# One transfer queue, two deadlines: the down part of an expert asked for behind the gate and up parts of the next

## The reference

```python
# MOE_EXPERTS = 32, MOE_TOP_K = 2, MOE_FF = 256, D_MODEL = 1024
combine = jnp.einsum('tk,tke->te', w, jax.nn.one_hot(flat_idx, MOE_EXPERTS))
gate = jnp.einsum('td,edf->tef', t, w_gate)      # w_gate (32, 1024, 256)
up   = jnp.einsum('td,edf->tef', t, w_up)        # w_up   (32, 1024, 256)
hid  = jax.nn.silu(gate) * up * combine[:, :, None]
out  = jnp.einsum('tef,efd->td', hid, w_down)    # w_down (32, 256, 1024)
```

## Times and profile before

| | us |
|---|---|
| median of 3 runs | 1007.43 |
| the 3 runs | 1004.38, 1007.43, 1034.75 |
| the profiled execution, its own time | 1007.99 |
| its span in the trace | 1005.8 |

### The profile page before, as it was taken

The page is one execution under the profiler, slowest core; times in us unless marked ns, Lnnn a source line. Parts: engine busy times, 40 slices in busy tenths (PEclk is TensorE's granted clock), DMA queues, the critical chain, the costliest instruction groups (busy, mean ns, idle before and its releaser), DMA issues.

```text
span 1005.8 us, 15290 instructions
## 1 busy us (share of the span) xinstructions
PE 961.0 (96%) x5525; PEld 577.3 (57%) x5525; DVE 512.6 (51%) x936; ACT 306.6 (30%) x599; POOL 217.9 (22%) x267
## 2 busy tenths in 40 slices
PE   7999999999989999998999999999999998999986
PEld 5544444444546656667666665576655555555552
DVE  2366446444865555556567776573333332333327
ACT  3220002222544434432232233133333333333313
POOL 2200000222600750001233332002222222222003
PEclk9999999999999999998999999999999999999999
DMA  9996523000000000005011114987999999999748
GB/s 324 359 353 223 208 92 53 0 1 0 7 0 1 1 1 1 2 1 210 1 64 63 63 64 190 410 317 251 371 418 404 403 400 384 417 415 405 267 181 334
DMA packets 55072, 192.54 MB, mean 191 GB/s; under 512 B 15370, under 2 KB 26706, under 8 KB 39506
## 3 DMA queue, kind: packets, MB, share of 16 engines
q1 hardware_dynamic: 46644, 173.10, 45.2%
q0 software_dynamic: 7056, 18.36, 4.8%
q10 hardware_dynamic: 1296, 0.07, 0.1%
HBM read 174.21 MB, written 24.64 MB: 198 GB/s over the span
## 4 chain that ended last, share of the span: by engine, by line
PE 43%; DMA 6%; DVE 3%; issue 1%; ACT 1%; SPq 0%; ACTq 0%; POOL 0%; DVEq 0%; POOLq 0%
PE PS L1671 13%; PE PS L1540 11%; PE PS L1697 7%; DMA ring<-in_w_down_dram 3%; PE PS L1646 2%; PE PS L1464 1%; PE PS L1562 1%; PE PS L1508 1%; DMA ring<-in_w_gate_dram 1%; PE PS L1728 1%; DMA y_g<-y_rows 1%; PE PS L1523 1%; PE PS L1680 1%; PE PS L1552 1%; DVE y_sum L2311 1%
## 5 line engine op out<-in xcount | busy, mean ns | idle before, releaser
L1671 PE MATMUL PS<-ring,xg_T 128*64 x736 | 162.7, 379 | 3.5 <-ACT near_gu L1857 2.6
L1671 PE MATMUL PS<-near_gu,xg_T 128*64 128x256 f32 x736 | 162.7, 379 | 0.0
L1671 PEld LDWEIGHTS PS<-ring,xg_T 128*64 128x64 f32 x736 | 100.7, 137 | 63.0 <-issue 16.3
L1540 PE MATMUL PS<-w_out_sb,cat_T 128*128 128x512 f32 x256 | 118.0, 603 | 1.4 <-DVE y_sc L2006 1.0
L1012 PE MATMUL PS<-hT,w_x 128*128 128x512 f32 x256 | 112.0, 594 | 0.0
L435 POOL TENSOR_SCALAR rstd<-stat 128x1 f32<-128x1 f32 (+1 forms) x48 | 22.3, 465 | 368.8 <-ACT junk L615 181.3
L1671 PEld LDWEIGHTS PS<-near_gu,xg_T 128*64 128x64 f32 x736 | 100.7, 137 | 0.0
L1697 PE MATMUL PS<-ring,hid_T 128*64 x184 | 83.8, 598 | 0.4 <-DVE hid_T L2253 0.4
L1697 PE MATMUL PS<-near_dn,hid_T 128*64 128x512 f32 x184 | 83.9, 598 | 0.0
L1012 PEld LDWEIGHTS PS<-hT,w_x 128*128 128x128 f32 x256 | 47.8, 190 | 58.1 <-issue 57.8
L916 DVE TENSOR_REDUCE row_max<-PS 128x1 f32<-128x1024 f32 (+7 forms) x64 | 48.2, 754 | 60.8 <-PE PS L1165 60.6
(11 more groups left out here) (342 smaller groups left out, 1562.1 us busy)
## 6 DMA issues: line engine op xcount, KB each, us to landing
ring<-in_w_gate_dram SPq DMA_DIRECT2D x32, 1024.0 KB, 11.1
ring<-in_w_up_dram SPq DMA_DIRECT2D x32, 1024.0 KB, 13.9
ring<-in_w_down_dram SPq DMA_DIRECT2D x32, 1024.0 KB, 16.3
ada_later<-in_ada_w_dram SPq DMA_DIRECT2D x16, 1024.0 KB, 4.8
ada_first<-in_ada_w_dram SPq DMA_DIRECT2D x16, 512.0 KB, 9.7
y_g<-y_rows SPq DMA_DIRECT2D x8, 1024.0 KB, 12.4
x_in<-in_x_dram SPq DMA_DIRECT2D x8, 512.0 KB, 7.8
w_out_sb<-in_w_out_dram SPq DMA_DIRECT2D x1, 4096.0 KB, 13.2
```

Of the source, the lines that this page charges most:

```text
L1540: last = pe.matmul(BANK[out_bank(t) + j], cat_T[t % 2][:, k, :], w_out_sb[:, k, j * HALF:(j + 1) * HALF], start=(k == 0), stop=(k == KC - 1))
L1671: last = pe.matmul(BANK[2 + s_][rows_, 0:FF], xg_T[b][:, k, rows_], gu[u][:, s_, k, :], start=(k == 0), stop=(k == KC - 1))
```

## The change

The loop over experts asks for a down part one pass later: pass e now issues the gate and up parts of expert e and then the down part of expert e-1. The arrivals are awaited and reported in a new order as well: pass e waits for gate and up of e-2 and for down of e-3. The down part waits for the same condition as before (`used_first` is the `used` of the pass before).

```diff
-                def landed(e):
-                    for part in "wud":
+                def landed(e, parts="wud"):
+                    for part in parts:
                         sp.wait_ge(S[f"{part}_loaded{e % RING}"], 16 * (e // RING + 1))
                         sp.sem_inc(S[f"{part}_ready"], 1)
...
-                for e in range(RING - 2):
+                for e in range(RING - 3):
                     landed(e)
+                landed(RING - 3, "wu")
...
                 for e in range(RING, E):
                     r = e % RING
-                    landed(e - 2)
+                    landed(e - 2, "wu")
+                    landed(e - 3, "d")
                     used = last_step(e - RING)
                     sp.wait_ge(S["gate_done"], used)
                     sp.wait_ge(S["near_gu_act"], used)
...
                     load_up(sp, e, r)
-                    sp.wait_ge(S["dn_done"], used)
-                    load_down(sp, e, r)
-                landed(E - 2)
-                landed(E - 1)
+                    if e > RING:
+                        sp.wait_ge(S["dn_done"], used_first)
+                        load_down(sp, e - 1, (e - 1) % RING)
+                    used_first = used
+                sp.wait_ge(S["dn_done"], used_first)
+                load_down(sp, E - 1, (E - 1) % RING)
+                landed(E - 2, "wu")
+                landed(E - 3, "d")
+                landed(E - 1, "wu")
+                landed(E - 2, "d")
+                landed(E - 1, "d")
                 used = last_step(E - RING + 2)
```

## The result

| | before | changed |
|---|---|---|
| median of 19 runs each, us | 1006.70 | 1012.98 |
| profiled execution, its own time, us | 1007.99 | 1012.34 |
| span of the profiled execution, us | 1005.8 | 1010.4 |

The ratio of the times is 1.0067, with a 95% interval from 1.0055 to 1.0078: slower by about 6.7 us, less than 1% (the ratio leaves out the one slow run of before, 1034.75 us). In the profiled executions the change costs 4.35 us. The forecast was 1012, with a range from 1004 to 1017 us.

A forecast was written before the change was run, and what follows sets the result against it. TensorE was taken to set the end, with one 2.6 us hole. The late down part gave +4.1 us, with the other spacing +5.0, the removed stall included; +4.5 on the median 1007.43 made 1012, range 1004 to 1017 us.

The forecast's parts named there:

- The bound: Over the steps, TensorE sets the end with one hole, the gate wait at step 13; at most 2.6 us to gain.
- Term 1: Start of the expert loop: the weight stream is not shifted or up to 1.3 us late; 0.3 us taken.
- rival B: Queue loses its start: whole weight stream 8.6 us late, down(13) +12.4 us, time 1020; chance 0.14.
- Term 2: SyncE's new waits do not drain the queue behind pass 8; cost and gain 0.
- Term 3: Step 13: gate of expert 21 lands at 838.5, so the stall goes, -2.6 us.
- Term 4: Step 13: down of expert 21 lands two places later, its down product at 856.3, +4.1 us, at the other spacing +5.0.
- The choice of 2.69 us a part: Around step 13, parts arrive 2.69 us apart with gathers kept away by the stall, not 3.12; sum +4.1, not +5.0.
- The 420 GB/s: Measured rate over the steps, taken to decide against a 358 GB/s read limit giving 3.7 us a part and +6.
- Term 5: Step 11: down of expert 18 comes late, a new 2.4 us stall that adds nothing to the sum.
- A: Step 13's gate comes early and its down part in time: -2.6 us, time 1004.8; chance 0.18.
- C: Parts queued together do not land in order, so places do not matter: time 1007; chance 0.05.

The follow-up runs named there:

- e1: Changed kernel, but down parts of experts 18 and 21 asked for at their old places, gate and up of 19 and 22 too; ratio 0.9992 to the kernel before.
- e7: Experts asked for in pairs: gate and up of two experts, then both down parts; ratio 1.0003 to the kernel before, median 1007.80 us.
- e4: Half the dose: against the kernel before, gate one place early, up unmoved, down one place late; ratio 0.9997.
- e10: The order with down parts of experts 18 and 21 put back, run again unchanged; ratio 0.9984 to the kernel before.
- e6: Double dose: down part asked for two passes later, four places behind its old one; ratio 1.0076 to the kernel before, median 1015.6 us.
- e2: Changed kernel, in steps 11 and 13 the down copy moved behind SiLU on ScalarE and behind the hidden product on VectorE; ratio 1.0050 to the kernel before.
- e3: Changed kernel with idle matmuls filling TensorE's holes, 9 in step 11 and 28 in step 13; ratio 1.0063 to the kernel before.
- e9: The kernel before, run again unchanged for a second profile; profiled execution 1004.86 us.

## Why the prediction was right, and where it was off

The forecast of +4.5 us met the profiled +4.35 us in part by luck: the stream came about 2 us earlier than I had it, and two terms that I did not have, 1.64 us of half clock behind the hole and 0.77 us behind the last step, made up for it.

- **The bound.** Right. TensorE sets the end, with one hole; e1 closed it and gave 2.8 us in the steps, about the limit that the prediction set (2.6 us in the list of waits).
- **Term 1, the start of the loop.** Mis-sized. I took the stream to be 0.3 us late; it was early. Gate of expert 7, alone in the queue, took 5.1 us to land, not the 6.3 us taken from u6. Gate of expert 8, the sixth part, landed 9.7 us after 705.48, at 715.1; before, the sixth part (d7) landed at 717.0. The steps also began 0.46 us earlier, so the stream was about 1.4 us ahead of the steps' clock. Gates landed 4 to 7 us earlier than before (g20 at 826.9 against 831.0, g25 at 870.6 against 877.7), not the 3 us of the forecast; down of expert 21 landed 3.6 us later, not 6. The fear of rival B, a lost start, had the wrong sign.
- **Term 2, SyncE's waits.** Right: no cost (e1).
- **Term 3, the gate hole.** Right: step 13 started at 841.78 with no wait for the copy, after a step 12 that was 1.4 us late itself (forecast 843.4).
- **Term 4, the late down part.** The mechanism was right to the row: the landing at 851.1 (forecast 853.2), 3.2 us of path (forecast 3.1), the down product at 854.3 (forecast 856.3). The difference of 2 us from 853.2 is the size of term 1; from the 854.1 of the other spacing it would be 3. The step counts +2.1 against +4.1.
- **The choice of 2.69 us a part.** Wrong for this part, and hidden by the error of term 1. Down of expert 21 landed only 2 us after TensorE had stopped, so the parts ahead of it came at the old spacing. In the third profile of the change up of expert 21 landed at 823.38 + 14.4 = 837.8 and its down part, four places behind, at 832.33 + 18.2 = 850.5: 3.2 us a part. The hole begins there only at 848.6. The parts behind it did come faster: gate of expert 24, again four places on, landed at 851.3 + 9.4 = 860.7, 2.5 us a part. In e1, which has no hole, the same four places took 3.0 us each (851.4 to 863.5). Between 850 and 860 us the queue of the weights moved 3.99 MB in the first profile of the change and 3.48 MB in e1, that of the gathers and scatters 0.10 and 0.59 MB. The Trainium skill, "DMA: Bandwidth & Descriptors", section "Queues, rings and completion order", has each engine take turns between its queues, and the trace agrees: the payback that I drew from it exists, but it comes behind the hole, too late for the part that made the hole.
- **The 420 GB/s.** The prediction sets them against a limit on reads, but they count reads and writes. The weights alone are 1.05 MB in 3.12 us, 336 GB/s. The argument was thinner than it looked; its result, about 3.1 us a part and not 3.7, held.
- **Term 5, step 11.** Right: a hole of 1.4 us (forecast 2.4), absorbed by the one in step 13. In e7, where nothing absorbs it, it counts.
- **What was missing: the clock.** The prediction gave a hole the price of its length. The 16 matmuls behind it cost 1.64 us more, and filling the holes gave back about 3 us over the runs (1.0067 against 1.0034). That is the likely reason why +4.5 came out as +6.7 in the ratio, and in the profile it made up for the error of term 1.

The profiled difference adds up: steps begin 0.46 us earlier, down(13) counted from there is 2.60 us later, half clock behind it 1.64, and the end of the kernel 0.77 us longer, 4.55 us of span. The last term is a stretch of 3.4 us at half clock near 970, present in the three profiles of the change, absent in both of before:

```profile
955.00:970.00 15.00, 11.40 (x84) 6.00 (x80) 4.95 (x13) 2.53 (x4) 1.99 (x2) 1.00 0.22 85
970.00:974.00 4.00, 3.82 (x19) 3.82 (x20) 0.12 (x1) 0.00 (x0) 0.00 (x0) 0.57 0.20 66
```

It lies where TensorE has been idle between the last step and the sums, for 2.8 us in every profile, with or without it. What puts it there isn't settled, and it does not go with the change's loss: apart from the two of before, every profile has a stretch there except e1's. That of e4 has one too, and e10, the same kernel as e1, has 6.8 us.

- **The rivals.** A (down part in time) and C (places do not matter) fell with the landings and with the doses of e4 and e6. B fell at the eighth part: it landed at 721.1 and 720.5 us in the second and third profile of the change (the first has no landing for it), against 722.8 before and the 726 that B asked for.

## What to carry to other kernels

In a queue that is never empty, asking for one thing earlier is asking for another later: write down the places, multiply by the measured spacing, and compare each arrival with its own deadline, not with the one that was late so far. The deadline of a copy is not its reader's start but the start of what stands behind it in the same engine's list. A hole of some microseconds in the matrix engine can cost a stretch at half clock besides its length. Before reordering, look which small set of transfers is late (here one gate part of 26) and move as little else as possible; that moving this one part alone would do was not run.

## What the runs showed of the hardware that was not expected

- Holes in TensorE and the clock behind them. The holes of 3.8 to 4.3 us in the three profiles of the change and of 3.8 us in e6 were each followed by 3.4 us at half clock, and so was one of 2.4 us in e6; in e2 the drop came inside a hole of 3.4 us. The gate holes of before, 2.6 and 2.3 us, were not, nor was any of 0.9 to 2.0 us in the steps. The hole of 2.8 us behind the last step stands in all 13 profiles: in ten the clock dropped in it or within 1.4 us behind it, in three it did not (both of before, and e1). The length of a hole alone does not tell.
- The time won by shortening a hole can go straight back to the clock: in e2 the down product of step 13 started 1.1 us earlier than in the change and the next step 0.06 us earlier, both counted from the start of step 0 (168.5 against 169.6 us, 174.65 against 174.71 us).
- One matmul call on these float32 tiles stands as two records, 0.223 us for both where the call is 128x128 by 128 columns; e3 was sized wrongly for that reason. A transpose stands as one (2 calls, x2, at L1689).
- The same kernel differs by 3 us between executions, mostly ahead of the steps, where one has stretches at half clock and the other none (e9: 1004.86 us with almost none, mean clock 0.999; the first profile 1007.99 us, 0.994).
